# Norm and input projection in one stage, index queries first, scores in fours, flags moved later

## What is computed

```
def trunk_layer(x, past, lw, lam_init, t5_table):
    topk = min(TOPK_MAX, L // 4)          # 256 for the prompt, 40 for the sample
    hn = rmsnorm(x, g_mix)
    parts = split_proj(jnp.einsum('btd,dn->btn', hn, w_in))
    # q, k, v of four head groups (sb, df, ds, fx), index queries q_ix (8 x 64), index key k_ix (64), weights w_ix (8), gates
...
    # in mix_block:
    s_ix = jax.nn.relu(jnp.einsum('bqhd,bkd->bqhk', q_ix.astype(f32), k_ix) * (IDX_DIM ** -0.5))
    score = jnp.einsum('bqh,bqhk->bqk', w_ix.astype(f32) * (N_IDX_HEADS ** -0.5), s_ix)
    score = jnp.where(chunk_ok, score, -jnp.inf)
    top_val, top_idx = lax.top_k(score, topk)   # the ds group attends to these keys only
...
    x = x + jnp.einsum('btm,md->btd', mixed.astype(x.dtype), w_out)
    # then a norm, a gated convolution MLP, and x + its product
```

## Time and profile before

| | us |
|---|---|
| median of 3 runs | 3903.53 (3903.22 to 3904.62) |
| the profiled execution | 3907.19 |
| its span, first to last instruction | 3905.4 |
| PE busy in the span | 3388.9 (87%) |
| DVE busy | 2494.5 (64%) |
| ACT busy | 1141.0 (29%) |
| POOL busy | 160.4 (4%) |

### The profile page before, as it was taken

How to read it: one execution, slowest core, us unless ns; L and a number is a source line. 1 busy time by engine, 2 the same in 40 slices (tenths; PEclk the granted TensorE clock), 3 DMA queues, 4 the chain that set the end, 5 groups by cost and what they waited for, 6 DMA issues and landing times. The chain is left out here.

```text
span 3905.4 us, 58909 instructions
## 1 busy us (share of the span) xinstructions
PE 3388.9 (87%) x21785; PEld 2945.4 (75%) x21785; DVE 2494.5 (64%) x5332; ACT 1141.0 (29%) x2365; POOL 160.4 (4%) x174
## 2 busy tenths in 40 slices
PE   3799892999988999999948999659999799999995
PEld 2688781656658999999947888535566699999994
DVE  3189887575754666655635988766656566665665
ACT  3222221564632111111132222235554311111112
POOL 0201100000000000000011101000000000000000
PEclk7899896998989999999968989879899899999997
DMA  4122222211001111111011222221100111111101
GB/s 143 48 69 81 75 67 76 81 57 48 22 11 60 49 48 35 46 48 48 11 35 55 84 66 80 99 81 61 46 12 24 44 49 38 43 48 48 48 27 46
DMA packets 229803, 210.78 MB, mean 54 GB/s; under 512 B 27430, under 2 KB 215494, under 8 KB 227550
## 3 DMA queue, kind: packets, MB, share of 16 engines
q1 hardware_dynamic: 229598, 208.10, 16.6%
HBM read 159.83 MB, written 44.91 MB: 52 GB/s over the span
## 5 line engine op out<-in xcount | busy, mean ns | idle before, releaser
L1684 PE MATMUL psum<-h_split,gate_up_split 128*128 128x352 f32 x6336 | 1019.9, 322 | 44.2 <-DVE gate_up_split L1798 44.2
L1684 PEld LDWEIGHTS psum<-h_split,gate_up_split 128*128 128x128 f32 x6336 | 1011.9, 188 | 48.2 <-issue 46.5
L1828 DVE TENSOR_TENSOR arena<-arena,psum 128x352 f32<-128x352 f32 x1056 | 513.7, 521 | 318.4 <-PE psum L1684 318.2
L1684 PE MATMUL psum<-hid_split,down_split 128*128 128x352 f32 x3168 | 523.2, 325 | 11.1 <-DVE down_split L1798 11.1
L1684 PEld LDWEIGHTS psum<-hid_split,down_split 128*128 128x128 f32 x3168 | 516.8, 190 | 11.6 <-issue 11.6
L854 PE MATMUL psum<-w_in_split,h_split 128*128 128x256 f32 x3456 | 442.8, 288 | 0.0
L854 PEld LDWEIGHTS psum<-w_in_split,h_split 128*128 128x128 f32 x3456 | 428.2, 193 | 14.4 <-issue 14.4
L1025 DVE TENSOR_SCALAR_CACHE_REDUCE flags<-arena,selection 32x160 uint8<-32x160 f32 (+6 forms) x448 | 386.8, 863 | 16.0
L1318 PE MATMUL psum<-arena 64*128 64x512 f32 (+9 forms) x1040 | 220.9, 529 | 159.1 <-DMA arena<-q_turned 138.5
L856 PE MATMUL psum<-h_split,w_in_split 128*128 128x352 f32 x1872 | 317.4, 333 | 45.9 <-POOL w_in_split L992 45.9
L856 PEld LDWEIGHTS psum<-h_split,w_in_split 128*128 128x128 f32 x1872 | 313.7, 197 | 51.7 <-issue 51.7
(11 more groups left out here) (159 smaller groups left out, 3049.6 us busy)
## 6 DMA issues: line engine op xcount, KB each, us to landing
w_in_raw<-in_w_in SPq DMA_DIRECT2D x28, 1024.0 KB
gate_up_raw<-in_w_gate SPq DMA_DIRECT2D x44, 512.0 KB, 3.7
gate_up_raw<-in_w_up SPq DMA_DIRECT2D x44, 512.0 KB, 4.7
down_raw<-in_w_down SPq DMA_DIRECT2D x44, 512.0 KB, 3.2
arena<-k_turned SPq DMA_DIRECT2D x8, 1184.0 KB, 5.8
k_turned<-arena SPq DMA_DIRECT2D x72, 128.0 KB, 2.1
q_turned<-arena SPq DMA_DIRECT2D x48, 176.0 KB, 1.8
arena<-bias_strips SPq DMA_DIRECT2D x4, 2048.0 KB, 10.4
```

The lines of the kernel that those rows point to most:

```text
L1684: ins = nc.tensor.matmul(out, w[i], x[k], start=(first and n == 0), stop=(last and n == 2))
L1828: nc.vector.tensor_tensor(x, x, bank(m, down_bank[p])[:, 0:PIECE], ALU.add).then_inc(s.added, 1)
```

## The change

- `stage_norm` is no longer called ahead of the projection. Its work is inside `stage_project`. PE now sums the squares itself, eight products with ones for each third of the tokens, and DVE scales and splits third by third (`normalize`). The parameters are loaded, turned and prepared in this stage too.
- The special piece and the two index pieces (`EARLY = 3`) have raw buffers and split buffers of their own and are loaded at the start. Their 15 products come by thirds of the tokens, five products to a third.
- Transposes use one PSUM bank (4) in place of two.
- Scores come in chunks of four units, one chunk between two products. The first chunk of a block is placed 10 us ahead of the time at which the plan has DVE free, the others after it. `block_time` and the durations of products have new numbers.
- In a round of `select` the compare writes its result to PSUM (`m.step_bits`, bank 5) and the next instruction reads it there.
- The sample block is selected by `select_few`: five times `max` and `match_replace`, then one comparison.
- All flags are left where the scores were, and the wait for `proj_done` before block 7 is gone. SP moves them at the start of `stage_attend`, between its first loads, and PE waits there for them.
- The loads for the attention's first group are issued before the last nine v products, not after them.

```diff
-    def lay_out(self, waiting):
-        plan, now, due, begun = self.plan, 0.0, 0.0, False
+        for i in range(3):
+            for pc in self.pieces[:EARLY]:
+                self.feature_major(pc, i)
...
+            if o.piece.i >= EARLY:
+                if not chunks and waiting and now >= free - 10:
+                    blk = waiting.pop(0)
+                    chunks = self.chunks_of(blk)
+                    plan.append(("score", chunks.pop(0)))
+                    now += 1.5
+                    due = free + SLACK_US
+                    free = max(free, now) + block_time(blk)
+                    begun = blk
+                elif chunks and now >= due:
+                    if begun.n == GATES_BLOCK:
+                        plan.append(("gates", begun))
+                        begun = BLOCKS[0]
+                    plan.append(("score", chunks.pop(0)))
+                    now += 1.5
...
+            rested += not waiting and not chunks
+            if rested >= 3 and o.o >= last_k and not loaded:
+                plan.append(("load", None))
+                loaded = True
...
+        return [(blk, us[i:i + RELU_RING]) for i in range(0, len(us), RELU_RING)]
```

```diff
@@ stage_project, tensor
+            def sum_squares(p):
+                for c in range(KC):
+                    i = p * KC + c
+                    pe.wait_ge(s.squared, i + 1)
+                    nc.tensor.matmul(bank(m, 4 + p)[:, 0:PIECE], m.ones[:, :], m.squares_mix[:, i % SQUARES, :],
+                                     start=c == 0, stop=c == KC - 1).then_inc(s.squares_added, 1)
...
+                if pc.kind == "special":
+                    pe.wait_ge(s.h_low, KC * (o.i + 1))
...
-                if t.i >= 2:
-                    pe.wait_ge(s.turn_kept, t.i - 1)
-                dst = bank(m, 4 + t.i % 2)
+                if t.i:
+                    pe.wait_ge(s.turn_kept, t.i)
+                dst = bank(m, 4)
...
+            sum_squares(0)
+            turn_params()
+            sum_squares(1)
+            sum_squares(2)
@@ scalar
+            for i in range(8):
+                square(i)
             high(0)
+            for i in range(8, 14):
+                square(i)
+            keep_params()
+            rstd(0)
+            for i in range(14, 16):
+                square(i)
+            for i in range(KC):
+                h_high(i)
+            high(1)
+            rstd(1)
+            for i in range(16, 24):
+                square(i)
+            high(2)
+            rstd(2)
+            for i in range(KC, 2 * KC):
+                h_high(i)
@@ vector
+            def normalize(p):
+                cols = slice(p * PIECE, (p + 1) * PIECE)
+                dve.wait_ge(s.rstd_ready, p + 1)
+                for c in range(KC):
...
+                    nc.vector.scalar_tensor_tensor(out=m.norm_ring_mix[:, i % NORM_RING, :], in0=m.xT[:, c, cols],
...
+                for c in range(KC):
+                    i = p * KC + c
+                    dve.wait_ge(s.h_high, i + 1)
+                    nc.vector.tensor_tensor(m.h_split[:, 1, c, cols], m.norm_ring_mix[:, i % NORM_RING, :],
...
-                cand_bits, step_bits = (m.pick_bits[0:n, i:i + 1] for i in (4, 5))
+                cand_bits, step_bits = m.pick_bits[0:n, 4:5], m.step_bits[0:n, :]
...
+            def select_few(blk, score):
+                top = m.top[0:blk.rows, :]
+                for _ in range(TOPK_SAMPLE // ROUNDS_OF_8):
+                    own(nc.vector.max(top, score))
+                    own(nc.vector.match_replace(out=score, in_to_replace=top, in_values=score, imm_value=TAKEN))
+                nc.vector.tensor_scalar(score, score, TAKEN / 2, None, ALU.is_gt).then_inc(s.selected, 1)
...
-                flags = score
-                if blk is SELECTED[-1]:
-                    dve.wait_ge(s.proj_done, len(proj))
-                    flags = taken_keys(m)[blk.n]
-                select(blk, score, flags)
@@ stage_attend
+            load_q(0)
+            move_flags(masked_blocks[0], s.first_flags_in)
+            for e in range(1, 3):
                 load_q(e)
+            for blk in masked_blocks[1:]:
+                move_flags(blk, s.flags_in)
...
+                    if blk is masked_blocks[0]:
+                        pe.wait_ge(s.first_flags_in, 16)
+                    if blk is masked_blocks[1]:
+                        pe.wait_ge(s.flags_in, 16 * (len(masked_blocks) - 1))
```

369 lines of the change are left out of this document (221 added, 148 removed).

## The result

The changed kernel takes 3797.6 us (median of four runs, 3787.6 to 3799.2) against 3903.99 us before (four runs, 3903.2 to 3904.6): a ratio of 0.9722, 95% interval 0.9705 to 0.9739. It is faster, and much less than forecast: 106 us instead of 180, and outside the range, which ended at 3785.

What follows compares the result with a forecast made beforehand. DVE's chain of weightings and selections, ending at 581, then a PE tail of some 4 us, bounds the stage; attention starts 90.0 us per layer earlier: 3905.4 - 2 x 90.0 = 3725.4, median 3724. Range 3705 to 3745 (0.50), 3680 to 3785 (near 0.85).

Steps and rivals of the forecast that it cites:

- Front: Norm and index products: first product at 93 us, index queries and keys at 160, DVE starting at 167 instead of 188.
- D: Rival, front: PE's sums and ACT's casts delay index queries to 180 as before; 20 us per layer, 3764; chance 0.04.
- Sample block: Head of DVE's chain: five max and match_replace pairs and a comparison take 5 us instead of 31 rounds; DVE free at 180.
- The round: Selection's count, compare, step: with one step input in PSUM, nine holds (34.6 us) per layer go; PSUM itself costs nothing.
- B: Rival, selection rounds: PSUM makes them quicker (-0.10 us each, 3693; chance 0.14) or dearer (+0.05, 3740; chance 0.08).
- Lengths of the selections: DVE's selections of blocks 2 to 7 without holds: 40.1 us at 384 keys to 65.7 at 1024, sum 317.
- rival A: Selections: steps still held, or POOL's splits hit other DVE instructions; about ten of 3.8 us, 38 per layer, 3800; chance 0.10.
- Weightings: Gaps from DVE free to each selection, fed at PE's pace: 7.5 us (384 keys) to 18.8 (1024), 83.5 in all.
- PE after the last meeting: Stage's end: from 496, PE's remaining chunks and products run to 585, so PE and SP's tail ends it some 4 us after DVE.
- C: Rival: stores behind the group load stall v products, or POOL holds the norm; 12 to 20 us per layer, 3750 to 3764; chance 0.12.
- Flags: Start of attention: six flag transfers, some 2 MB, stay hidden behind the first queries; otherwise up to 5 us per layer.
- E: Rival, projection: PE's clock stays low behind its stops; 103 us per layer, slower than before at 3930; chance 0.02.

Runs made afterwards that it cites:

- loads ahead: Changed kernel with each weight piece loaded some four products after the start of the piece two before it: 3727.9 us; same edit on the kernel before: 3873.1 us.
- the one bank alone: Kernel before the change with one PSUM bank instead of two for the projection's transposes, step still in SBUF: 3946.4 us, ratio 1.0108.
- the chunks in a row: Kernel with loads ahead, a block's score chunks after the first placed one behind another without projection products between: 3722.2 us, ratio 0.9541.
- the one with quarters: Changed kernel with POOL's 128x2048 weight split done in four instructions of 128x512: 3766.3 us, ratio 0.9658.

## Why the prediction was wrong

**What bounds: right but for the tail.** DVE's chain of selections sets the end, before with the wait for the last product on top. Attention starts when block 7 is selected; the forecast had PE's tail end the stage some 4 us behind that.

**Front: right.** First product, first score and first weighting are within 1.5 us. D is out. That ACT is held there by a load was said in the forecast, as a thing that stays; with the loads ahead the front is 10 us per layer shorter, and it was the first sight of what follows.

**Sample block: right.** 4.0 us for 5, and the stage that the block heads keeps 20 of the 25.4 us that it gives.

**The round: right.** Steps at 158 ns, none held, and with the step back in SBUF nine holds return. B is out on both sides: a [128,1] operand in PSUM costs nothing as an input, and as the output of the compare 8 ns (222 for 214). By the errata table of the Trainium skill ("VectorE: DVE Perf Modes", section on the TRN2 errata) the step would have been 65 ns dearer, an estimate from its two fixed costs; the trace (158 ns against 159) doesn't agree.

**Lengths of the selections: failed by 16.2, and it is rival A in part.** "POOL's splits hit other DVE instructions" was in its condition, with 38 us per layer and a chance of 0.10. Against it stood that count and compare are never held, which is still so. But behind the rounds stand five instructions on whole rows of keys, and four of the twelve splits met one of them (14.8 us). The forecast had taken the lengths from the selections of 384 and 1024 keys less their holds at L1036 (and without holds they are right: 318.4 us with the loads ahead, 317.1 forecast) and didn't ask which other instructions can be held. Its argument against A was that instructions with one tensor input are never held, and the trace of before already showed one that is: L1073 in the earlier trace rows, a `TENSOR_SCALAR` of 32x160, takes 4.36 us at 187.79, under this split:

```profile
187.56 4.50 POOL L992 TENSOR_TENSOR w_in_split<-w_in_raw,w_in_split 128x2048 fp32r<-128x2048 f32 x1 [18.25 <-ACT w_in_split L923]
```

The forecast carried that hold along inside the 7.7 us of the sample's weighting. The traces show such holds on scalar_tensor_tensor with two SBUF inputs (4.83), on the scan with two (5.54 in layer 1 at 2204.06), and on `TENSOR_SCALAR` with one wide input (5.04 above), never on the counting form with its accumulator (192 per layer, 946 ns on average, the same with and without holds elsewhere) nor on the [128,1] compare. The Trainium skill has a rule that fits: by "SBUF — State Buffer", section "SBUF: two separate sides", VectorE and GpSimd share a pair of ports under an exclusive lock for a whole instruction, and the VectorE side is either a two-port mode or two SBUF inputs. The forecast used the second half of that condition only. The trace agrees with the second half (4.83, 5.54) and fits the first: `TENSOR_SCALAR` with a wide input is held (5.04), and unheld it takes 0.48 us for 128x512, where `SCALAR_TENSOR_TENSOR` takes 0.84.

**Weightings: failed by 24.6, the larger share.** The gaps were put together from PE's products and chunks as if PE always had them ready and at full clock. One term left out is what PE waits on ACT: 18.9 us at the v pieces, 3 to 4.5 at each k piece, 7.7 where a chunk stands right behind a piece. The wait of 3.9 at a k piece was in the earlier trace rows and was used once, in the tail, where it costs nothing; it occurs at every k piece (14.2 us in four waits). The one bank for transposes was costed at the ten small ones of the front and not at the v pieces, where it turns ACT's 6 us in the DMA wait into a stall of PE. The experiments size this term: loads ahead take 10.0 us off the gaps and 10.0 off the front; before the change the one bank alone costs 19. The other 14.6 us stay when the stalls are gone. They are the sum itself, which was too short for five of the six blocks. The forecast gives its gaps without their terms, but for block 7 its prices (three chunks of 3.35 and two q products of 3.85) make 17.75 of its 18.8. In the trace with the loads ahead these stretches take 19.6, of which 1.4 is low clock behind PE's stop, and the two ends, before PE's first and after its last score, 3.3 where 1.05 was left for them. For the other blocks the surplus was not taken apart. That the products between the chunks make these gaps long is shown: with the chunks in a row they are 20.2 us shorter.

**PE after the last meeting: the order held, the end didn't decide.** PE's last product ended at 618.2, some 3 us ahead of DVE. ACT's stop behind stores that wait for the group load came as C says (9.6 us in three waits of L1028), under that cover.

**Flags: right.** No wait of attention for them; the first attention score starts 3.5 us after DVE's end, as before (3.4).

**E** is out as a verdict: the granted clock was 0.90 instead of 0.92 in the projection, and the kernel is faster. Its mechanism is there in small: behind PE's stop ahead of block 7 a chunk and a product take 8.8 us at 0.60, the next such pair 7.4 at 1.00 (both with the loads ahead).

The range ended at 3785, below A's 3800, and the measured 3797.6 lies next to A's figure by chance: the price of A was worked out for all holds together or none, and the case that came true, a third of the splits on other instructions together with a PE that is late, wasn't listed.

## What to carry to other kernels

Where an engine that empties PSUM also casts weights, look at its wait for the load: all that stands behind it in its queue waits as well, and try issuing each load as soon as its buffer is free; in the two kernels here where that was tried it only gained. A saving on the engine that bounds shows only as far as the engine that feeds it is early at each meeting, so sum the feeder's own waits (on banks and on others' queues) before adding up its products, and check such a sum on a gap of the old trace. When one kind of instruction is freed from a hold, list every other that can be held before booking the gain. And when an edit moves one engine, look at what else moved before putting the time down to it: here POOL's splits met other DVE instructions from one kernel to the next, and that was worth up to 15 us per layer.

## What the hardware did that was not expected

Cut into four, POOL's split and DVE's wide instructions take turns: three DVE instructions in a row at 1.5 to 1.6 us in place of one at 4.8, and POOL's quarter takes 1407 ns on average, more than a quarter of the 4667 of the whole. Where nothing is held (at 208.00) four quarters take 5.00 us.

In attention there is a stretch in which the clock may or may not fall. Three rows of 60 us, the first two from the same place of layer 0 (180 us behind DVE's end) in the changed kernel and in the one with quarters, the third from layer 1 of the changed kernel:

```profile
801.20:861.20 60.00, 52.78 (x371) 33.93 (x367) 37.62 (x104) 33.95 (x94) 0.00 (x0) 0.80 0.09 27
```

```profile
798.90:858.90 60.00, 51.85 (x437) 33.01 (x437) 41.47 (x123) 38.92 (x111) 0.00 (x0) 0.98 0.15 46
```

```profile
2644.30:2704.30 60.00, 51.84 (x420) 32.50 (x420) 42.06 (x123) 39.65 (x111) 0.00 (x0) 0.97 0.11 32
```

With a granted clock of 0.80, a mix of 2.4 and 1.2 GHz, PE does 371 matrix instructions there; at 0.97 or 0.98 it does 420 and more. In all three the 60 us ahead had 54.6 us of PE busy at 0.99 or 1.00, and the code is the same. From DVE's end in layer 1 to the end of the kernel the changed kernel took 1321.5 us in this execution and 1331.7 before the change, where that stretch was low (0.79 in layer 0, 0.82 in layer 1). So one such fall is worth some 10 us there, and 16 between the changed kernel and the one with quarters in layer 0. It would account for the 10 us by which the profiled execution is below the three others (their mean clock is 0.937 or 0.938, its own 0.943; they have no trace), and for most of the 31 us of the kernel with quarters, whose profiled execution had no fall in either layer. What decides whether it comes was not tested and stays open; differences of under 10 us per layer are therefore read here from DVE's times within the stage and not from medians.
